# RWKV chunks of a hybrid decoder step: the far product and the turned tokens are issued behind the first squares

## The reference

```python
z = jnp.einsum('btd,dp->btp', hn, p['w_in'])
...
y_c, rw_shift, rw_S = _rwkv7_branch(z_rw, rw_shift, rw_S, p)
...
def step(S, inp):
    r_t, w_t, k_t, v_t, kk_t, a_t = inp
    sa = jnp.einsum('bhvk,bhk->bhv', S, -kk_t)
    S = (S * w_t[:, :, None, :] + sa[..., None] * (kk_t * a_t)[:, :, None, :]
         + v_t[..., None] * k_t[:, :, None, :])
    return S, jnp.einsum('bhvk,bhk->bhv', S, r_t)
```

## Time and profile before

| | us |
|---|---|
| median of three runs | 2070.17 |
| the profiled execution | 2067.74 |
| its span, first to last instruction | 2065.9 |
| TensorE busy | 2038.5 (99%) |
| GpSimd busy | 1451.1 (70%) |
| ScalarE busy | 765.1 (37%) |
| VectorE busy | 705.1 (34%) |
| RWKV chunks, from the first near product to the last chunk's states | about 532 to 795 |

### The profile page before, as it was taken

One profiled execution on the slowest core, in us unless ns is written; L12 is line 12 of the kernel. 1 busy time (PEld: TensorE's weight loads), 2 busy tenths in 40 slices (PEclk: granted clock), 3 DMA queues, 4 the chain that ended last, 5 costly groups with the idle time before them and its releaser, 6 DMA issues.

```text
span 2065.9 us, 39851 instructions
## 1 busy us (share of the span) xinstructions
PE 2038.5 (99%) x15918; PEld 2005.0 (97%) x15918; DVE 705.1 (34%) x1117; ACT 765.1 (37%) x942; POOL 1451.1 (70%) x1104
## 2 busy tenths in 40 slices
PE   9999999999999999999999999999999999999997
PEld 8999999999999999999999999999999999999997
DVE  5667646683422225356314511111000111111112
ACT  6354343544222223333335533333333333333332
POOL 7787765697755555778776777777777777777774
PEclk9999999999999999999999999999999999999999
DMA  7656555654433443677543444444544444444542
GB/s 255 208 173 205 200 190 184 202 169 163 153 130 122 129 133 119 195 251 248 213 148 126 154 144 156 147 144 153 148 150 153 148 146 154 147 146 148 151 150 97
DMA packets 130983, 338.24 MB, mean 164 GB/s; under 512 B 14896, under 2 KB 59036, under 8 KB 130496
## 3 DMA queue, kind: packets, MB, share of 16 engines
q1 hardware_dynamic: 113008, 315.07, 47.3%
q10 hardware_dynamic: 17872, 21.70, 2.9%
HBM read 312.84 MB, written 23.88 MB: 163 GB/s over the span
## 4 chain that ended last, share of the span: by engine, by line
PE 54%; POOL 25%; issue 19%; DVE 1%; ACT 1%; POOLq 0%; DVEq 0%
POOL w_lo L1483 25%; PE banks_g L1514 16%; PE banks_g L1512 16%; PE banks_g L1513 16%; PE banks_g L1645 1%; PE banks_g L1646 1%; PE banks_m L1646 1%; PE banks_m L1645 1%; PE banks_g L1647 1%; PE banks_m L1647 1%; DVE banks_m L2215 0%; DVE banks_m L2189 0%; POOLq L1477 0%; ACT x_hi L1990 0%; POOLq L1481 0%
## 5 line engine op out<-in xcount | busy, mean ns | idle before, releaser
L1483 POOL TENSOR_TENSOR w_lo<-w_raw,w_hi 128x512 fp32r<-128x512 f32 (+1 forms) x1096 | 1444.8, 1343 | 594.6 <-ACT w_hi L1937 263.8
L1512 PE MATMUL banks_g<-x_hi,w_hi 128*128 128x320 f32 x3168 | 989.9, 312 | 2.0 <-POOL w_lo L1483 1.6
L1514 PE MATMUL banks_g<-x_hi,w_lo 128*128 128x320 f32 x3168 | 979.9, 309 | 0.0
L1513 PE MATMUL banks_g<-x_lo,w_hi 128*128 128x320 f32 x3168 | 979.8, 309 | 0.0
L1512 PEld LDWEIGHTS banks_g<-x_hi,w_hi 128*128 128x128 f32 x3168 | 595.6, 188 | 9.1 <-issue 2.4
L1513 PEld LDWEIGHTS banks_g<-x_lo,w_hi 128*128 128x128 f32 x3168 | 596.0, 188 | 0.6
L1514 PEld LDWEIGHTS banks_g<-x_hi,w_lo 128*128 128x128 f32 x3168 | 595.8, 188 | 0.0
L1818 ACT ACTIVATE w_hi<-w_raw 128x1024 fp32r<-128x1024 f32 (+1 forms) x248 | 258.1, 1041 | 246.6 <-PE banks_g L1514 243.4
L1937 ACT ACTIVATE w_hi<-w_raw 128x1024 fp32r<-128x1024 f32 x188 | 197.2, 1057 | 381.4 <-PE banks_g L1514 349.2
L1512 PE MATMUL banks_g<-a_hi,w_hi 128*128 128x320 f32 x704 | 217.4, 309 | 0.0
L1514 PE MATMUL banks_g<-a_hi,w_lo 128*128 128x320 f32 x704 | 217.4, 309 | 0.0
(11 more groups left out here) (380 smaller groups left out, 1756.2 us busy)
## 6 DMA issues: line engine op xcount, KB each, us to landing
w_raw<-in_w_f SPq DMA_DIRECT2D x211, 512.0 KB, 3.8
w_raw<-in_w_fi SPq DMA_DIRECT2D x176, 512.0 KB, 3.6
w_raw<-in_w_fo SPq DMA_DIRECT2D x64, 512.0 KB, 3.5
front_scratch<-ev ACTq DMA_DIRECT2D x106, 160.0 KB, 3.0
w_raw<-in_w_br SPq DMA_DIRECT2D x32, 512.0 KB, 4.7
w_raw<-in_w_o SPq DMA_DIRECT2D x32, 512.0 KB, 3.6
arena<-front_scratch SPq DMA_DIRECT2D x25, 640.0 KB, 5.8
w_raw<-in_w_fo SPq DMA_DIRECT2D x32, 384.0 KB, 3.0
```

Of the source, the lines that this page charges most:

```text
L1483: low = nc.gpsimd.tensor_tensor(w_lo[:, q % RING, c0:c1], w_raw[:, q % RING, c0:c1], w_hi[:, q % RING, c0:c1].bitcast(F32), ALU.subtract)
L1512: pe.matmul(out, wh, hi[:, k0 + k, :], start=first and k == 0, stop=False)
L1513: pe.matmul(out, wh, lo[:, k0 + k, :], start=False, stop=False)
L1514: mm = pe.matmul(out, wl, hi[:, k0 + k, :], start=False, stop=last and k == tiles - 1)
```

## The change

The 32 products of `C_far` are issued behind the first squares instead of behind the near products, with the same bank and the same place in the sequence of that bank's uses. VectorE's two evictions of them are moved likewise, behind those of the first squares. No instruction is added or taken away, and `fill` puts the same numbers of pieces at the same places.

```diff
@@ -582,11 +582,6 @@
                 heads(pair, 1, (Bt, At, 0, 1))
                 heads(pair, 2, (Bt, Rt, 0, 1))
                 closed(heads(pair, 3, (Kt, Rt, 0, 1)), "C_near")
-                pair = opened("C_far")
-                heads(pair, 0, (Kt, At, 0, 1))
-                for slot, x in ((1, Bt), (2, Kt), (3, Vt)):
-                    mm = heads(pair, slot, (x, eye, 0, 1))
-                closed(mm, "C_far")
 
                 fill(("C_QI", n), 2)
                 pe.wait_ge(S("C_QI"), n + 1)
@@ -596,6 +591,11 @@
                     heads(pair, 0, (eye, of(h_T), 1, 0))
                 heads(pair, 1, (of(h_Q), of(h_N), 1, side))
                 closed(heads(pair, 2, (of(h_N), of(h_Q), 1, side)), "C_p2")
+                pair = opened("C_far")
+                heads(pair, 0, (Kt, At, 0, 1))
+                for slot, x in ((1, Bt), (2, Kt), (3, Vt)):
+                    mm = heads(pair, slot, (x, eye, 0, 1))
+                closed(mm, "C_far")
                 fill(("C_2", n), 1)
                 was_read(pe, "C_p2", n)
                 pair = opened("C_p4")
@@ -1307,9 +1307,6 @@
                 masked(h_masked, near, 2, "maskS" if smp else "iT").then_inc(read(*near), 1)
                 sync()
                 put(tt(h_T, h_Q, bc(K("ident2"), 1, 4), ALU.add), "C_QI", n + 1)
-                full(dve, *late)
-                link(masked(h_ak, late, 0, "nT_seq" if smp else "sT"))
-                copied(h_turned, late, 1).then_inc(read(*late), 1)
                 full(dve, "C_p2", n)
                 was_read(dve, *near)
                 link(one_more(h_E, ("C_p2", n), 1))
@@ -1317,6 +1314,9 @@
                     put(copied(h_powers, ("C_p2", n), 1), *use("C_p2", n))
                 else:
                     put(copied(h_levels, ("C_p2", n), 0), *use("C_p2", n))
+                full(dve, *late)
+                link(masked(h_ak, late, 0, "nT_seq" if smp else "sT"))
+                copied(h_turned, late, 1).then_inc(read(*late), 1)
                 full(dve, "C_p4", n)
                 link(one_more(h_E, ("C_p4", n), 1))
                 put(copied(h_levels, ("C_p4", n), 0), *use("C_p4", n))
```

## The result

The changed kernel takes 2058.97 us in the median of six runs (2058.23 to 2060.74), the kernel before 2069.85 us in six (2065.93 to 2071.26). The ratio is 0.9950, with a 95% interval of 0.9940 to 0.9961: 10.9 us, or 0.5%, faster. The forecast was 2061.1 us in a range of 2058 to 2066. The gain lies under 2%, but both the interval and the two sets of runs, which don't overlap, are clear of no change.

The account below looks back on a forecast made before the run. TensorE, busy 99%, was taken as the bound, losing 9.04 us to three seam gaps and lower clock. 2065.9 - 9.0 = 2056.9, plus 1.84 gives 2058.7, plus 2.43 to the median: 2061.1 us, range 2058 to 2066.

Parts of the forecast that it names:

- The gaps are code that has not arrived: First three seams between chunks: TensorE's code comes in blocks of 256 instructions, the next late; gaps cost 6.20 us.
- Rival 3: Gaps belong to the transposes, the products that read `con`, and move along with them; then 2070 us; chance 0.08.
- The semaphore of the far group: Seam runs: `opened` waits for banks 2 and 3 ahead of the far product; ruled out as the gaps' cause.
- The price of the three seams, 9.04 us: Seams between chunks 0 and 3: gaps of 6.20 us plus 2.84 us of lower clock, all to be saved.
- the moved 64 records cost the same there: Run of first squares, grown from 48 records to 112: the moved records cost 0 us more there.
- The longer run of first squares costs nothing: First squares in each chunk: taken as 0 us; bounds 0 and one gap with its lower clock, 3.67 us.
- the 0.1 us to spare: Chunk 2's first squares, the worst block: passed in 4.3 us against at most 4.17 for the next block's arrival.
- The rule: TensorE's code blocks: one passed in less than about 3.8 to 4.2 us ends in a gap.
- Rivals 1 and 4: One or two gaps stay or arise (2062.6 to 2064.8); lower clock behind first squares (up to 2063.9); together 0.14.
- VectorE's side at 0 us, cover 2.0 us: Far group's evictions behind the first squares: DVE done 2.0 us before `C_p4` falls due, cost 0.
- Rival 2: `C_p4` waits for DVE in every chunk: five waits with lower clock, 14 us against 9 gained, 2075; chance 0.04.
- the sum's 2058.7: Profiled execution of the changed kernel: 2056.9 us of span plus the 1.84 us around it.

Follow-up runs that it names:

- the first shift of the code: The kernel before with 48 more instructions in TensorE's list ahead of its first product, nothing moved in the chunks: 2066.94 us against 2070.96 (0.9976).
- two repeats of TensorE's order: The kernel before with only VectorE's two evictions moved (2067.55 us against 2068.35), and the kernel before once more, unchanged (one time, 2069.45 us).
- the second shift: The kernel before with 156 more instructions in TensorE's list ahead of its first product, no product of a chunk moved: 2062.80 us against 2070.96 (0.9963).
- the cut: The kernel before with one of the two pieces behind the far group put between near products and far group: 2060.35 us against 2070.96 (0.9943).
- e11_before_again: The kernel before once more, unchanged, on the same chip: one time of 2069.45 us.
- the two shifts by 48 instructions: 48 more instructions ahead of TensorE's first product, in the kernel before (2066.94 us) and in the changed kernel (2059.22 us), each against 2070.96.
- both halves alone: Changed kernel with DVE's two evictions back ahead of the first squares: 2058.97 us; kernel before with only these evictions moved: 2067.55; each against 2068.35.
- VectorE's half: The kernel before with only DVE's two far-group evictions moved behind the first squares: 2067.55 us against 2068.35 (0.9996).

## Why the prediction was right

- **The gaps are code that has not arrived.** Shown. They keep to a grid of 256 instructions through the first shift of the code, two repeats of TensorE's order and a run of 448 products with nothing between them; one comes in the middle of the stream's products; and their length follows the packet of code when the weight load is held back. The transposes are innocent: they run unchanged, without a gap, in the second shift and in the cut. Rival 3 is out. The semaphore of the far group is out too, since it is waited for unchanged in the second shift.
- **The price of the three seams, 9.04 us.** The chunks gave 9.56 us. The periods were forecast at 50.32 us and are 50.15, so 0.5 us more over three: a term that the sum had at nothing ("the moved 64 records cost the same there"). The two runs together take 2.03 + 1.79 = 3.82 us, where the undisturbed seam and the squares took 3.13 + 0.86 = 3.99. In the trace of the kernel before the excess stands at one place, between records 128 and 129 of the seam, where the far product begins: in the fourth seam they start 0.16 us apart, where the step from one product to the next is 0.04. DVE's L1299, which reads `C_o` out of PSUM, ends at 742.90 there, and record 129 starts at 742.96. Chunk 0, with no `C_o` ahead, has no such step. So it is most likely a short wait of the far group for `C_o`'s eviction; this is read from the trace, no run tests it.
- **The longer run of first squares costs nothing.** Right, but by a rule that lacked a part. By an estimate from the places with and without a gap (34 and 48) and from the packets' starts, the block is asked for while TensorE is still about 48 instructions ahead of the old block's end, here in stream products, which take some nine times as long per instruction as the small ones. So chunk 2 had more than the 0.1 us to spare that I gave it. The rule was at odds with a row on record already: in the fourth seam of the kernel before, the block from instruction 149 to 405 is passed in some 3.4 us by the earlier trace rows and would have had to end in a gap, which that execution doesn't show and `e11_before_again` does (0.87 us). The missing part made the times expected of the two shifts by 48 instructions too high, and had me expect gaps in the second shift that did not come. Rivals 1 and 4 did not come.
- **VectorE's side at 0 us, cover 2.0 us.** 1.9 us measured, and both halves alone confirm the 0 us. Rival 2 did not come.
- **The median.** It fell by 10.9 us where the profiled executions differ by 8.8 and the sum said 9.0. The forecast carried the 2.43 us by which the median before lies above its profiled execution over to the changed kernel. There they are 0.03 us: this term was mis-sized, and it makes up the 2.1 us by which the forecast is too high. The kernel before has a share that changes from execution to execution: how many gaps are followed by the lower clock (two in the first profile, one in that of `e11_before_again`), and whether the fourth seam pays. Its runs on these chips spread from 2063.4 to 2073.9 us. Those of the changed kernel, which has no gap, lie within 2.5 us. That the profiled execution came out 0.2 us from the sum's 2058.7 is partly luck: 0.5 us more in the chunks and 1.0 us behind them are set against 1.75 us lost ahead.
- **The page on the fetch.** The blocks of 256 instructions are as the Trainium skill ("Runtime: NRT & Kernel Launch", section "Instruction fetch mechanics") says. That the fetch is mostly hidden because issue is slower than the fill does not hold for products of 64 x 64, which pass a block in 2.0 us against 3.5 to 4.6 for its arrival. The measurement decides.

## What to carry to other kernels

A wait put down to "issue", inside a long run of short instructions and at a place that drifts from one repeat to the next, is worth a count of instructions: if the places are 256 apart, the engine runs out of code. Then spread the short instructions among long ones so that no stretch of some 300 instructions takes under 3.5 us (4.6 with weight loads in flight); this is an estimate from the arrivals above and the 48 instructions of lead. Where work cannot be moved, moving the load or the code's place can give a good part of the same: holding back the loads gave 6 us, the two shifts 4 and 8, the change 11. A comparison of two kernels can be off by that alone, when an edit elsewhere changes the number of instructions ahead.

## What was not expected of the hardware

- Shifting the code by 156 instructions, with all products of the chunks in place, gave 8 us of 2071; holding back four weight loads gave 6 us.
- With a weight load of 512 KB issued at the seam, the packet of code starts up to 1.1 us later (2.2 against 1.0 us behind the run's start).
- A gap of 1.88 us was followed by 3 us at a granted clock of 0.54 in the first profile and by none of it in that of VectorE's half. Nor does the longer gap bring it: in the first shift the gap of 2.60 us was followed by 1.00 and that of 1.83 us by 0.50. Behind gaps of 1.10 us and less no slow matmul was seen.
